# Differential attention with maxima of half rows, both maps combined on GpSimd, and V held stationary for two query tiles

## Chip, core, metric

The kernel runs on one core of one Trainium2 chip. The metric is the device time of one execution in microseconds, given as the median of several runs. In what follows TensorE is the matmul engine (PE, and PEld for its weight loads), VectorE is DVE, ScalarE is ACT, GpSimd is POOL, and SyncE (SP) issues the transfers. SBUF is the on-chip memory of 128 partitions, PSUM the smaller one that TensorE writes to; GpSimd doesn't work on PSUM.

## What is computed

One layer of an encoder over 2048 tokens of width 1024: a projection, differential attention with 4 heads, dilated attention with 8 heads, an output projection, an MLP and a gate. The change concerns the differential attention:

```python
def block(qblk):
    s = jnp.einsum('bhmqd,bhmkd->bhmqk', qblk.astype(jnp.float32) * scale, kf)
    pr = jax.nn.softmax(s, axis=-1)
    a = pr[:, :, 0] - lam * pr[:, :, 1]
    return jnp.einsum('bhqk,bhkd->bhqd', a, vf)
...
o = rms_norm(o, subln_g, SUBLN_EPS) * (1.0 - lam_init)
```

`m` counts the two maps of a head, `scale` is 64 ** -0.5, keys are 2048, and `vf` has 128 columns for a head.

## The kernel before

The kernel is a list of six phases, each with its own on-chip tiles and a barrier behind it. Every engine has its own program, written out by hand; the engines meet only at semaphores (`wait_ge`, `then_inc`), and each runs its program in order. Float32 products are made from halves: a value is split into `hi` (a rounded copy, on ScalarE) and `lo` (the rest, a subtraction on VectorE), and two or three products of halves are added (`matmul3`). Each product has its own load of the stationary operand.

`project_phase` ends with the query stage: it turns queries and keys (`products` on VectorE, `rope` on GpSimd, L368, two inputs in SBUF), splits them (`qk_hi` on ScalarE, L262; `qk_lo` on VectorE, L326, two inputs in SBUF) and stores both halves.

`differential_phase` has 64 steps (`STEPS`), one for each tile of 128 queries of each head; head by head, 16 tiles each. K and V of two heads are held, and queries for 8 tiles twice. Step `n` does this:

- TensorE: `score` makes the scores of a map, 128 queries by 2048 keys, into four PSUM banks of 512 (L753, L754), 8 products a map. The four banks are shared by all maps, so a map's banks are written again when ScalarE has read them.
- VectorE: `maximum` (L623) reduces 1024 columns of PSUM, twice a map; `negate` (L628) joins the two and multiplies by -scale.
- ScalarE: `exp` (L563) exponentiates 1024 columns, with the whole row's maximum as bias, into `e` in SBUF, and gives the sum of each half row.
- VectorE: `denominators` (L634), `reciprocals` (L640) and `coefficient` (L645, minus lambda times the ratio of the denominators); `combine` (L660) makes `a_row` = e of map 1 x coefficient + e of map 0 over 2048 columns, two inputs in SBUF.
- TensorE: `turn_a` (L763) transposes `a_row` in four groups of four blocks into two PSUM banks; `a_hi` on ScalarE (L570) and `a_lo` on VectorE (L666, one input in PSUM, one in SBUF) split each group and free its bank.
- TensorE: `values` (L775, L776) holds a block of the turned weights stationary and moves V's two halves side by side (256 columns) past it, 32 products a tile.
- ScalarE `part` (L577), VectorE `result` (L672), ScalarE `square` and `unit`, GpSimd `root` (L720 to L724, a power of one column) and `finish` (L730) scale and normalise the 128x128 result. SyncE stores it.

The stages overlap: scores of tile n+1 and n+2, the turning of tile n and the values of tiles n-1 and n-2 stand in one turn of TensorE's loop. The order of VectorE's loop is the one to follow: maximum of the next tile, denominators, `a_lo` of the tile before, reciprocals, maximum, coefficient, negate, `a_lo`, combine, maximum, maximum, negate, `a_lo`, `a_lo`, result, keep.

## Time and profile before

| | us |
|---|---|
| runs (3): median | 3828.11 |
| runs: lowest, highest | 3823.57, 3841.12 |
| profiled execution, its own time | 3841.16 |
| its span | 3839.0 |
| differential stage within the span, from its first transfer to the next stage's | 623.4 to 1421.6 |

| engine | busy us, whole span | share |
|---|---|---|
| TensorE | 3455.9 | 90% |
| VectorE | 1928.7 | 50% |
| ScalarE | 1337.9 | 35% |
| GpSimd | 663.8 | 17% |

A row of a timeline has the start, the length, the engine, the line, the operation and its tiles (out<-in, partitions x elements); behind it in brackets the idle time before it and what ended that. "x2" is two instructions in one row. An operation's start can lie a little before the end of its predecessor, because they are pipelined. Rows of groups have the count, the busy time, the mean length in ns, and the idle time before them. A "granted clock" of 1 is 2.4 GHz, 0.5 is 1.2 GHz.

### The profile page before, as it was taken

The numbers are of one execution on the slowest core, as the hardware profiler recorded it, in microseconds if no ns is written. First come the engines' busy times: TensorE is split into PE (matmuls) and PEld (weight loads), VectorE is DVE, ScalarE is ACT, GpSimd is POOL, SyncE is SP. The second block draws the span as 40 slices with busy tenths as digits, with TensorE's granted clock in tenths as the row PEclk, the third lists the DMA queues.
The fourth block names the chain that finished last, engine by engine and source line by source line (L and its number), as shares of the span: only waits on it lengthen the run. The fifth ranks groups of instructions, "written<-read, shape, count | busy, mean of one in ns | idle before, by whom it ended". The sixth has DMA issues, their size and how long they took to land. (4 is left out here: it accounts for less than half of the span.)

```text
span 3839.0 us, 51498 instructions
## 1 busy us (share of the span) xinstructions
PE 3455.9 (90%) x18272; PEld 2965.2 (77%) x18272; DVE 1928.7 (50%) x3626; ACT 1337.9 (35%) x2814; POOL 663.8 (17%) x760
## 2 busy tenths in 40 slices
PE   5999995888888869999489799999999999998698
PEld 5998884777777759999377688888888888887587
DVE  3214442889989958888344333333343333332333
ACT  3211111666666647776122221112221112111333
POOL 2013331011111110000121121122211222111122
PEclk8999997999999989999699899999999999999899
DMA  3333336212210026774454511111141111112332
GB/s 128 134 108 121 121 115 168 53 37 64 57 44 18 7 66 161 165 165 111 154 173 158 197 44 55 44 55 44 44 159 44 55 44 44 54 44 74 132 107 93
DMA packets 276374, 351.12 MB, mean 91 GB/s; under 512 B 74608, under 2 KB 204528, under 8 KB 270960
## 3 DMA queue, kind: packets, MB, share of 16 engines
q1 hardware_dynamic: 276208, 348.97, 30.5%
q8 instruction: 96, 1.57, 0.2%
q14 instruction: 70, 0.57, 0.1%
HBM read 247.86 MB, written 101.06 MB: 91 GB/s over the span
## 5 line engine op out<-in xcount | busy, mean ns | idle before, releaser
L1582 DVE TENSOR_TENSOR e_h<-e_down_acc,e_h 128x512 f32<-128x512 f32 x512 | 350.7, 691 | 850.1 <-PE e_down_acc L89 850.1
L87 PE MATMUL e_up_acc<-e_xt_hi,e_up_hi 128*128 128x512 f32 x1024 | 399.8, 390 | 20.7 <-DVE e_xt_lo L1559 20.7
L88 PE MATMUL e_up_acc<-e_xt_lo,e_up_hi 128*128 128x512 f32 x1024 | 399.5, 390 | 0.0
L89 PE MATMUL e_up_acc<-e_xt_hi,e_up_lo 128*128 128x512 f32 x1024 | 399.3, 390 | 0.0
L87 PE MATMUL e_down_acc<-e_down_hi,e_u_hi 128*128 128x512 f32 x1024 | 398.3, 389 | 0.0
L88 PE MATMUL e_down_acc<-e_down_lo,e_u_hi 128*128 128x512 f32 x1024 | 398.3, 389 | 0.0
L89 PE MATMUL e_down_acc<-e_down_hi,e_u_lo 128*128 128x512 f32 x1024 | 398.3, 389 | 0.0
L623 DVE TENSOR_REDUCE c_mx<-c_scores 128x1 f32<-128x1024 f32 x256 | 306.1, 1216 | 73.2 <-PE c_scores L754 73.2
L563 ACT ACTIVATE c_e<-c_scores,c_neg_max 128x1024 f32<-128x1024 f32 x256 | 283.4, 1113 | 87.9 <-DVE c_neg_max L628 87.9
L1602 POOL TENSOR_TENSOR e_sq<-e_r 128x512 f32<-128x512 f32 x128 | 133.7, 1045 | 1008.4 <-ACT e_r L1538 1008.4
L753 PE MATMUL c_scores<-c_kt_hi,c_qs 128*128 128x512 f32 x512 | 220.8, 431 | 51.1 <-DMA c_gain_in<-g_subln_dram 37.0
L775 PE MATMUL c_pv<-c_v_hl,c_at_hi 128*128 128x256 f32 x1024 | 249.3, 285 | 0.9 <-issue 0.9
L1532 ACT CAST e_down_hi<-e_down_raw 128x2048 fp32r<-128x2048 f32 x32 | 61.2, 1913 | 539.7 <-PE e_down_acc L89 538.1
L776 PE MATMUL c_pv<-c_v_hl,c_at_lo 128*128 128x256 f32 x1024 | 242.9, 280 | 0.0
L87 PEld LDWEIGHTS e_up_acc<-e_xt_hi,e_up_hi 128*128 128x128 f32 x1024 | 192.9, 188 | 61.6 <-issue 21.1
L763 PE MATMUL c_turned<-c_ident,c_a_row 128*128 128x128 f32 x1024 | 148.7, 279 | 101.2 <-DVE c_at_lo L666 100.1
L1047 PE MATMUL b_scores<-b_kt,b_qs 128*128 128x256 f32 x768 | 206.0, 400 | 25.6 <-DMA b_masks<-masks_dram 25.6
L763 PEld LDWEIGHTS c_turned<-c_ident,c_a_row 128*128 128x128 f32 x1024 | 121.6, 143 | 133.3 <-issue 115.5
L89 PEld LDWEIGHTS e_up_acc<-e_xt_hi,e_up_lo 128*128 128x128 f32 x1024 | 192.9, 188 | 40.2
L88 PEld LDWEIGHTS e_up_acc<-e_xt_lo,e_up_hi 128*128 128x128 f32 x1024 | 192.9, 188 | 40.1
L89 PEld LDWEIGHTS e_down_acc<-e_down_hi,e_u_lo 128*128 128x128 f32 x1024 | 192.2, 188 | 39.9
L88 PEld LDWEIGHTS e_down_acc<-e_down_lo,e_u_hi 128*128 128x128 f32 x1024 | 192.2, 188 | 39.9
(164 smaller groups left out, 7822.7 us busy)
## 6 DMA issues: line engine op xcount, KB each, us to landing
s_qkt<-a_hl SPq DMA_DIRECT2D x128, 256.0 KB, 2.8
e_up_raw<-w_up_dram SPq DMA_DIRECT2D x32, 1024.0 KB, 5.8
e_down_raw<-w_down_dram SPq DMA_DIRECT2D x32, 1024.0 KB, 4.9
s_v<-a_hl SPq DMA_DIRECT2D x64, 256.0 KB, 2.0
b_kt<-s_qkt SPq DMA_DIRECT2D x64, 256.0 KB, 10.9
a_w_raw<-w_in_dram SPq DMA_DIRECT2D x24, 512.0 KB, 5.6
d_nd<-s_nd SPq DMA_DIRECT2D x48, 256.0 KB, 4.2
a_rot<-x_dram SPq DMA_DIRECT2D x16, 512.0 KB, 3.8
```

What stands on the lines that cost most here:

```text
L87: nc.tensor.matmul(out, lhs_hi, rhs_hi, start=first, stop=False)
L88: nc.tensor.matmul(out, lhs_hi, rhs_lo, start=False, stop=False)
L89: return nc.tensor.matmul(out, lhs_lo, rhs_hi, start=False, stop=last)
L563: nc.scalar.activation(e[:, s, m, f * HALF:(f + 1) * HALF], scores[:, 2 * f:2 * f + 2].rearrange("p b k -> p (b k)"), ACT.Exp, bias=neg_ma ...
L623: nc.vector.tensor_reduce(mx[:, f:f + 1], scores[:, 2 * f:2 * f + 2].rearrange("p b k -> p (b k)"), AX.X, ALU.max).then_inc(S["mx"], 1)
L753: nc.tensor.matmul(scores[:, b], queries, kt_hi[:, h % 2, m, cols], start=True, stop=False)
L763: ins = nc.tensor.transpose(turned[:, g % 2, c * P:(c + 1) * P], a_row[:, n % 2, (4 * g + c) * P:(4 * g + c + 1) * P], ident[:])
L775: nc.tensor.matmul(pv[:, :2 * VD], at_hi[:, s, c], v, start=(c == 0), stop=False)
L776: ins = nc.tensor.matmul(pv[:, :2 * VD], at_lo[:, s, c], v, start=False, stop=(c == KT - 1))
L1047: ins = nc.tensor.matmul(dst, queries, keys, start=(u == 0), stop=(u == 1))
L1582: nc.vector.tensor_tensor(h[:, slot(z, t), cols], down_acc[:, k % 4], h[:, slot(z, t), cols], ALU.add).then_inc(S["h"], 1)
L1602: nc.gpsimd.tensor_tensor(sq[:, k % 2], r[:, k % 2], r[:, k % 2], ALU.mult).then_inc(S["sq"], 1)
```

## The change

- Each half row (1024 keys) of each map has its own maximum, negated by the reduction itself (`negate=True`), and is exponentiated with it at once. Afterwards the half rows are brought to the row's maximum by factors: `top_of` and `below_top` on VectorE, `correct` on ScalarE (an exponential of four columns), then `parts`, `denominators`, `reciprocals`, `shares`, `coefficients` on VectorE. The units are taken in the order map 0 and 1 of the first half, then of the second (`UNITS`).
- The factors (correction, one over the denominator, one or minus lambda) are multiplied in on GpSimd: `scale`, four times a tile over 128x1024 in place, and `combine`, twice a tile, e0 = e0 + e1 over 128x1024. For this there are three tiles of e for map 0 and two for map 1; `a_row` is gone.
- `values` handles two query tiles: V's halves are stationary and the weights of both tiles (256 columns) move, 48 products for two tiles. The result comes out turned; `o_out` on ScalarE copies it, `turn_back` on TensorE turns it, `square` and `root` (for both tiles at once) and `result` on VectorE normalise it, which also multiplies by the gain.
- V has one buffer, loaded by quarters; the queries are loaded for 4 tiles at a time; the first head's keys come in two halves.
- The factor 64 ** -0.5 is multiplied into the queries as they are split in `project_phase` and is left out of the exponentials, in the dilated phase and in the mixing too.
- TensorE's, ScalarE's and VectorE's loops are interleaved by quarters of a tile.

The core of the diff:

```diff
+            return (SCALE, 1.0)[QK_PAIRS[i // BLOCKS][2]]
...
+                        nc.scalar.activation(hl[:, 2 * ab], prod[:, 2 * ab], ACT.Copy, scale=factor(i)).then_inc(rope_hi, 1)
...
+                        nc.vector.scalar_tensor_tensor(out=hl[:, 2 * ab + 1], in0=prod[:, 2 * ab], scalar=factor(i),
+                                                       in1=hl[:, 2 * ab].bitcast(F32), op0=ALU.mult, op1=ALU.subtract
+                                                       ).then_inc(rope_lo, 1)
...
+    UNITS = tuple((m, f) for f in range(2) for m in range(2))
...
+                        sp.wait_ge(S["pv"], 8 * (h * PAIRS - 1) + 2 * g + 2)
...
+                    m, f = UNITS[u]
+                    act.wait_ge(S["negmax"], 4 * n + u + 1)
+                    if m == 0 and n >= 3:
+                        act.wait_ge(S["a_turned"], 4 * (n - 3) + 2 * f + 2)
+                    if m == 1 and n >= 2:
+                        act.wait_ge(S["a"], 2 * (n - 2) + f + 1)
+                    b = (4 * n + u) % 2
+                    nc.scalar.activation(e_of(n, m, f), scores[:, 2 * b:2 * b + 2].rearrange("p b k -> p (b k)"),
+                                         ACT.Exp, bias=neg_max[:, n % 2, m, f:f + 1],
+                                         accum_out=sums[:, n % 2, m, f:f + 1]).then_inc(S["exp"], 1)
...
+                    act.wait_ge(S["below"], n + 1)
...
+                                         below[:].rearrange("p m f -> p (m f)"), ACT.Exp).then_inc(S["corr"], 1)
...
+                for n in range(-2, STEPS + 4):
+                    j = n // 2 - 2
+                    closing = n % 2 == 0 and 0 <= j < STEPS // 2
+                    for q in range(4):
+                        if 0 <= n < STEPS:
+                            a_hi(n, q)
+                        if closing and q == 0:
+                            o_out(j)
+                        if n + 2 < STEPS:
+                            exp(n + 2, q)
+                        if closing and q >= 2:
+                            square(j, q - 2)
+                    if n + 2 < STEPS:
+                        correct(n + 2)
...
+                    nc.vector.tensor_reduce(neg_max[:, n % 2, m, f:f + 1],
+                                            scores[:, 2 * b:2 * b + 2].rearrange("p b k -> p (b k)"),
+                                            AX.X, ALU.max, negate=True).then_inc(S["negmax"], 1)
+                def top_of(n):
+                    dve.wait_ge(S["negmax"], 4 * n + 4)
+                    dve.wait_ge(S["below"], n)
+                    nc.vector.tensor_tensor(top[:], neg_max[:, n % 2, :, 0], neg_max[:, n % 2, :, 1],
+                                            ALU.min).then_inc(S["top"], 1)
+                def below_top(n):
+                    dve.wait_ge(S["top"], n + 1)
+                    dve.wait_ge(S["corr"], n)
+                    nc.vector.tensor_tensor(below[:], top[:].unsqueeze(2).to_broadcast([P, 2, 2]), neg_max[:, n % 2],
+                                            ALU.subtract).then_inc(S["below"], 1)
+                def parts(n):
+                    dve.wait_ge(S["corr"], n + 1)
+                    dve.wait_ge(S["den"], n)
+                    nc.vector.tensor_tensor(part[:], corr[:, n % 2], sums[:, n % 2], ALU.mult).then_inc(S["part"], 1)
...
+                    nc.vector.tensor_tensor(den[:], part[:, :, 0], part[:, :, 1], ALU.add).then_inc(S["den"], 1)
...
+                    nc.vector.tensor_tensor(share[:], rec[:], weights[:], ALU.mult).then_inc(S["share"], 1)
...
+                    nc.vector.tensor_tensor(coef[:, n % 2], corr[:, n % 2], share[:].unsqueeze(2).to_broadcast([P, 2, 2]),
...
+                    nc.vector.scalar_tensor_tensor(out=out[:, s], in0=o[:, s * P:(s + 1) * P], scalar=rstd[:, s:s + 1],
+                                                   in1=gain[:], op0=ALU.mult, op1=ALU.mult).then_inc(S["out"], 1)
...
+                    for q in range(4):
+                        if n + 2 < STEPS:
+                            maximum(n + 2, q)
+                        if chained:
+                            if q == 0:
+                                parts(n + 1)
+                            if q == 1:
+                                shares(n + 1)
+                        if 0 <= n < STEPS:
+                            a_lo(n, q)
+                        if chained:
+                            if q == 0:
+                                denominators(n + 1)
+                                reciprocals(n + 1)
+                            if q == 1:
+                                coefficients(n + 1)
+                        if closing and q < 2:
+                            result(j, q)
+                    if n + 2 < STEPS:
+                        top_of(n + 2)
+                        below_top(n + 2)
...
+                def scale(n, m, f):
+                    pool.wait_ge(S["coef"], n + 1)
+                    nc.gpsimd.tensor_scalar(e_of(n, m, f), e_of(n, m, f), coef[:, n % 2, m, f:f + 1], None,
+                                            ALU.mult).then_inc(S["scaled"], 1)
+                def combine(n, f):
+                    pool.wait_ge(S["scaled"], 4 * n + 3 + f)
+                    nc.gpsimd.tensor_tensor(e_of(n, 0, f), e_of(n, 0, f), e_of(n, 1, f), ALU.add).then_inc(S["a"], 1)
...
+                    nc.gpsimd.tensor_scalar(mean[:], ssq[:], 1.0 / VD, SUBLN_EPS, ALU.mult, ALU.add).then_inc(S["mean"], 1)
...
+                    nc.gpsimd.tensor_tensor(rstd[:], mean[:], half[:], ALU.pow).then_inc(S["rstd"], 1)
...
+                    if 0 <= n + 1 < STEPS:
+                        scale(n + 1, 0, 0)
+                        scale(n + 1, 1, 0)
+                        scale(n + 1, 0, 1)
+                        combine(n + 1, 0)
+                        scale(n + 1, 1, 1)
+                    if n % 2 == 0 and 0 <= j < STEPS // 2:
+                        root(j)
+                    if 0 <= n + 1 < STEPS:
+                        combine(n + 1, 1)
...
+                        pe.wait_ge(S["a_lo"], 4 * (2 * j + 1) + k // 2 + 1)
+                    for c in range(2 * k, 2 * k + 2):
+                        hi, lo = (t[:, s, c].rearrange("p s t -> p (s t)") for t in (at_hi, at_lo))
+                        ins = matmul3(nc, pv[:, :2 * P], v_hl[:, c, 0], v_hl[:, c, 1], hi, lo, c == 0, c == KT - 1)
...
+                    for q in range(4):
+                        if n + 2 < STEPS:
+                            score(n + 2, q)
+                        if 0 <= n < STEPS:
+                            turn(n, q)
+                        j = (n - 2) // 2
+                        if 0 <= j < STEPS // 2 and n >= 2:
+                            values(j, 4 * (n % 2) + q)
```

The functions that are replaced stand in the kernel printed above.

## Rows read from the trace of the kernel before

**Rows 1.** Busy time by engine, columns as headed, in the even middle of the stage.
```profile
core 0: us, PE busy (x) PEld busy (x) DVE busy (x) ACT busy (x) POOL busy (x), PEclk, DMA share, GB/s
700.00:1380.00 680.00, 583.03 (x3794) 497.54 (x3793) 613.64 (x952) 451.62 (x951) 90.80 (x236) 0.99 0.14 35
```

**Rows 2.** Timeline of VectorE over one step: start, length, line, operation, idle before.
```profile
1002.45 1.23 DVE L623 TENSOR_REDUCE c_mx<-c_scores 128x1 f32<-128x1024 f32 x1 [0.85 <-PE c_scores L754]
1003.59 0.15 DVE L634 TENSOR_TENSOR c_den<-c_sums 128x2 f32<-128x2 f32 x1
1003.65 0.68 DVE L666 TENSOR_TENSOR c_at_lo<-c_turned,c_at_hi 128x512 fp32r<-128x512 f32 x1
1004.25 0.15 DVE L640 RECIPROCAL c_rec<-c_den 128x2 f32<-128x2 f32 x1
1004.33 1.20 DVE L623 TENSOR_REDUCE c_mx<-c_scores 128x1 f32<-128x1024 f32 x1
1005.45 0.26 DVE L645 TENSOR_SCALAR c_coef<-c_den,c_neg_lam,c_rec 128x1 f32<-128x1 f32 x1
...
1012.32 0.34 DVE L672 SCALAR_TENSOR_TENSOR c_o<-c_pv,c_rec,c_o_part 128x128 f32<-128x128 f32 x1
...
1013.79 1.23 DVE L623 TENSOR_REDUCE c_mx<-c_scores 128x1 f32<-128x1024 f32 x1 [0.84 <-PE c_scores L754]
```

**Rows 3.** Waits of TensorE, 660 to 1400 us: total, times, longest.
```profile
PE c_turned L763 <- DVE c_at_lo L666: 100.1, 64, 1.6
```

**Rows 4.** Timeline of TensorE: scores, turns and values, to be read by starts.
```profile
703.75 0.40 PE L753 MATMUL c_scores<-c_kt_hi,c_qs 128*128 128x512 f32 x1
...
705.25 0.60 PE L763 MATMUL c_turned<-c_ident,c_a_row 128*128 128x128 f32 x4
705.60 0.37 PE L775 MATMUL c_pv<-c_v_hl,c_at_hi 128*128 128x256 f32 x1
...
705.92 0.28 PE L775 MATMUL c_pv<-c_v_hl,c_at_hi 128*128 128x256 f32 x1
706.04 0.28 PE L776 MATMUL c_pv<-c_v_hl,c_at_lo 128*128 128x256 f32 x1
```

**Rows 5.** Groups of ScalarE by shape, 620 to 1425 us: count, busy us, mean ns, idle.
```profile
L563 ACT ACTIVATE c_e<-c_scores,c_neg_max 128x1024 f32<-128x1024 f32 x256 | 283.4, 1113 | 87.9 <-DVE c_neg_max L628 87.9
```

**Rows 6.** Groups of GpSimd by shape, whole span: count, busy us, mean ns, idle.
```profile
L1602 POOL TENSOR_TENSOR e_sq<-e_r 128x512 f32<-128x512 f32 x128 | 133.7, 1045 | 1008.4 <-ACT e_r L1538 1008.4
...
L362 POOL TENSOR_TENSOR a_w_lo<-a_w_raw,a_w_hi 128x1024 fp32r<-128x1024 f32 x24 | 57.6, 2422 | 130.8 <-ACT a_w_hi L233 130.8
...
L356 POOL TENSOR_TENSOR a_rstd<-a_mean,a_half 128x1 f32<-128x1 f32 x16 | 8.8, 551 | 1.3
...
L351 POOL TENSOR_SCALAR a_mean<-a_ssq 128x1 f32<-128x1 f32 x16 | 3.1, 192 | 88.9 <-ACT a_junk L240 88.7
L1013 POOL MEMSET b_kt<- 128x1024 f32 x2 | 1.9, 952 | 3.1 <-POOLq L1948 3.0
```

**Rows 7.** Query stage: GpSimd's and VectorE's timelines, and L326's durations, min/median/max.
```profile
440.90 2.56 POOL L368 TENSOR_TENSOR a_prod<-a_prod 128x512 f32<-128x512 f32 x2 [8.32 <-DVE a_prod L319]
...
442.89 1.95 DVE L326 TENSOR_TENSOR a_hl<-a_prod,a_hl 128x512 fp32r<-128x512 f32 x2 [0.86 <-ACT a_hl L262]
...
L326 DVE TENSOR_TENSOR a_hl<-a_prod,a_hl x64: 692/889/1122, 279.7 to 618.2; 128x512 fp32r<-128x512 f32 x64
```

**Rows 8.** Timelines near the stage's end: VectorE's combining operation, GpSimd's power.
```profile
1383.86 2.34 DVE L660 SCALAR_TENSOR_TENSOR c_a_row<-c_e,c_coef 128x2048 f32<-128x2048 f32 x1
...
1384.13 2.48 POOL L724 TENSOR_TENSOR c_o_rstd<-c_o_mean,c_half 128x1 f32<-128x1 f32 x1
```

**Rows 9.** Timelines at the kernel's start: GpSimd's long pair, VectorE reading PSUM and SBUF.
```profile
11.39 5.28 POOL L362 TENSOR_TENSOR a_w_lo<-a_w_raw,a_w_hi 128x1024 fp32r<-128x1024 f32 x2 [0.56 <-ACT a_w_hi L233]
...
14.55 1.29 DVE L297 TENSOR_TENSOR a_xt_lo<-a_turned,a_xt_hi 128x512 fp32r<-128x512 f32 x2 [2.41 <-ACT a_xt_hi L246]
```

**Rows 10.** Busy times, granted clock, DMA at the stage's start (columns as rows 1).
```profile
623.00:651.00 28.00, 0.00 (x0) 0.00 (x0) 0.00 (x0) 0.00 (x0) 0.16 (x3) 0.50 0.98 210
```

## What the change should do to the time

> **What bounds the kernel now.** Only the differential stage (623 to 1421 us of the span of 3839.0) changes in its structure, so I read it alone: first busy time by engine, then one step of the bound engine, then who waits for it. In the even middle VectorE is busy 614 of 680 us, TensorE 583, ScalarE 452, GpSimd 91, at a granted clock of 0.99 [rows 1]. A step (one query tile of one head; there are 64) lasts 1013.79 - 1002.45 = 11.34 us by the start of its first maximum. In it VectorE idles once, 0.85 us, for scores [rows 2]; these come late because TensorE waits up to 1.6 us a step, 64 times, for the split of the turned weights on VectorE [rows 3]. So VectorE sets the step: 10.5 us of work and a loop through TensorE.
>
> I cost by starts, since neighbours overlap: a maximum 1005.45 - 1004.33 = 1.12 us, a split (c_at_lo) 1004.25 - 1003.65 = 0.60, a small independent operation 0.06 to 0.08, one that needs its predecessor's result its whole 0.15; a 128x128 scaling 0.34 long, some 0.26 [rows 2].
>
> **VectorE, its own work.** The combination over 2048 columns goes (2.34 us long [rows 8]), with the old coefficient, negations, copy and o. The four maxima and four splits stay: 4 x 1.12 + 4 x 0.60 = 6.9. Seven small operations come in their place (minimum of the half maxima, difference, parts, denominators, reciprocals, shares, coefficients): about 0.75. The final scaling is 0.26 for each tile. Sum 7.9 us, 2.6 below the 10.5 of now.
>
> **TensorE.** Scores are unchanged: six of them with a bank change took 705.25 - 703.75 = 1.50, so 16 take 4.0. Four turns take 0.35 (705.25 to 705.60), so 16 take 1.4. A 256-column product costs 706.04 - 705.92 = 0.12. Today 32 of them serve a tile; with V stationary 48 serve two tiles, so 24 a tile: 2.8 instead of 3.7 [rows 4]. With changes of kind in each quarter and the turns back, 9 us. Loads of V as stationary cost nothing more: there is one for each product now too. ScalarE loses two scalings of o, gains one copy per pair and an exponential of four columns; at 452 of 680 us, 7.5 a step, it has room [rows 1].
>
> **GpSimd.** This is what is new. It gets four scalings of 128x1024 in place by a per-partition number, and two additions of 128x1024. The addition has a row, the two-input subtraction of this size: 2.42 us on average, of which I use 2.40. A wide operation with one input has none. Lower end: the memset of this size, which only writes, 0.95. Upper end: 2.40 as for two inputs. Between them, squaring multiplies a tile with itself and reads it twice: (1.045 - 0.19) / 512 = 1.67 ns a column; read once, half of that, is 0.83, which is also the memset's rate. So I take 0.19 + 0.85 = 1.06, near the lower end [rows 6]. The sum is 4 x 1.06 + 2 x 2.40 = 9.0, with gaps 9.2, and every second step the root of the norm (0.19 + 0.55 and gaps, 0.9 with its wait) [rows 6]. 9.7 on average is more than TensorE's 9, and still below 11.34.
>
> **What GpSimd does to VectorE.** In the query stage GpSimd works from 440.90 to 443.46. VectorE's subtraction, both inputs in SBUF, starts at 442.89 and the pair ends at 444.84; of a pair one takes 0.69, the other 1.12 (the least and the most of that line). 442.89 + 1.12 = 444.01 = 443.46 + 0.55: it stood until GpSimd's instruction ended [rows 7]. The other way round, GpSimd's power of one column, begun at 1384.13 inside the combination that ran until 1386.20, lasted 2.48 [rows 8] instead of 0.55 [rows 6]. But two subtractions with one input in PSUM took an undisturbed 1.29 inside GpSimd's 11.39 to 16.67 [rows 9]. So an operation of VectorE that reads two SBUF tiles, and one of GpSimd that reads SBUF, exclude each other for whole instructions; maxima, splits and the final scaling (PSUM plus SBUF) don't. The Trainium skill (SBUF — State Buffer, Who interferes with whom) says so: an exclusive lock, held for a whole instruction, and only the shared ports contend; these rows agree. It makes no exception for small operations.
>
> The old stage had GpSimd almost empty. In the new one it works 9 us in a row, and six of VectorE's seven small operations read two SBUF tiles: all but the reciprocals. Behind each, in VectorE's order, stand the maxima, and behind these the exponentials, the next scores and everything else. One step, from the start of the coefficients at 0, which release GpSimd:
> - GpSimd: three scalings 0.26 to 3.44, addition from 3.52 to 5.92.
> - VectorE: maximum, split, maximum, split until 3.52; the minimum finds the addition and stands until 5.92, ends 6.07.
> - GpSimd's fourth scaling 6.07 to 7.13; the difference, which needs the minimum, stands until 7.13, ends 7.28. Maximum until 8.40.
> - GpSimd's second addition 7.28 to 9.68; parts stands until 9.68, ends 9.83. Split, denominators, reciprocals until 10.7; maximum 11.8, shares, split, and the next coefficients at 12.5.
>
> That is 7.9 of work (less the final scaling) and 4.8 of standing, partly in place of the idling of now. TensorE fits in: its four quarters of some 2.3 us need an exponential from two quarters before, 1.1 us long [rows 5]; the latest ends at 12.7, for scores (1.0) that are wanted at 14.2. The root adds 0.9 in every second step (it comes before the second addition), the final scaling 0.26 in the others: 13.1 on average. At 3.52 two requests fall together; if the minimum comes just ahead of the addition, the same layout gives 12.0, with the extras 12.6. I take the middle, 12.85.
>
> **The sum.** (12.85 - 11.34) x 64 = +97 us. The stage's start: for 28 us TensorE does nothing, since it waits for transfers of some 5 MB at 210 GB/s [rows 10]; half the first queries (0.5 MB) come later, -2 us. The 16 smaller key loads cost only issue time on SyncE's queue, which is ahead of the landings. V, now in one buffer, is reloaded by quarters of 0.5 MB at three changes of head, 2.4 us each at that rate, more than a step ahead of its use; uncovered, 3 x 10 us. In SyncE's queue these loads stand behind the stores of tiles that were done a step before, and the next keys behind them have 12 steps. The new waits of ScalarE for a free tile of weights concern tiles two and three steps old; its `correct` waits for the difference, so until 7.3 in the layout, and behind it the next turned group and exponential, which VectorE wants from 9.8 and allows from 8.4. The scale moved into the query stage rides on operations that are there anyway: the subtraction stays one pass, and VectorE idles there (0.86 ahead of it alone [rows 7]). Nothing for it, nor for the exponentials.
>
> The profiled execution took 3841.2 us, 13 above the median 3828.1. Its sum is 3841.2 + 95 = 3936, which is 3923 on the median.
>
> **Rivals.**
> - *Small operations aren't held* (the other side). If operations of two or four columns slip in, GpSimd's own 9.7 sets the step, with the loop through TensorE at most 10.3: 3828 - 64 x 1.35 = about 3740. For it: no row shows so small a two-input operation of VectorE beside a long one of GpSimd. Against it: the power of one column was held. It decides at 3.4 us of standing a step (11.34 - 7.9): below that the kernel is faster. 0.15.
> - *Held, but absorbed.* If TensorE paces VectorE anyway (9 against 7.9) and the small operations fall into GpSimd's gaps, two of three stands go and the step comes out where it is, 11.0 to 11.7: 3805 to 3850. 0.1.
> - *The wide scaling is slow.* At the rate of two reads, 0.19 + 1.70 = 1.89 us, GpSimd has 12.4 + 0.45 by itself and the layout, done again, gives 14.2, with the extras 14.7: +215, 4040. The Trainium skill (GPSIMD Engine Reference, 3.1 Elementwise) gives 1.03 cycles an element for short bodies, but 1.8 as the best of another loop, at 1.2 GHz: estimates of 0.9 and 1.5 us; by the latter the total would be near 4010. No row shows which. 0.15.
> - *The clock falls.* In the 28 us of waiting the granted clock was 0.50 [rows 10], which is 1.2 of 2.4 GHz. TensorE would be busy 9 of 12.85 against 583 of 680 now [rows 1]. Its idle pieces are below 3 us, so I give the long fall little: at half clock its 9 become 17, and 64 x 5.5 = +350. 0.03, within the tail.
>
> **How the numbers follow.** My forecast (held, narrow scaling, step 12.0 to 13.5, so 3868 to 3964) has 0.57: 3923. The range takes in the slow scaling above and most of the absorbed case below: 3815 to 4060. Half a per cent, 19 us, is about what can be told from no change. Faster: 0.15 and a third of the absorbed case, 0.18. Same: 0.05. Slower: 0.77.
>
> **What would show it.** VectorE's small two-input operations would show lengths of 1 to 2.5 us instead of 0.15, each ending just after an instruction of GpSimd; the reciprocals would stay at 0.15. GpSimd's scalings 1.06, additions 2.40. The products with V would number 1536 instead of 2048, and TensorE would wait for exponentials. Step near 12.85. I am wrong if these lengths are 0.15, or if GpSimd idles less than 2 us a step.

## The result and the profile after

The changed kernel took 4257.9 us (median of 4 runs, 4254.6 to 4261.0) against 3829.4 for the kernel before on the same chip: a ratio of 1.110, 95% interval 1.109 to 1.112. It is slower, as forecast, but by 428 us where I had said 95 (step 12.85 instead of 11.34), and outside the range. The profiled execution has a span of 4252.8 us. The difference lies in the differential stage: from 280 to 620 us, ahead of it, TensorE was busy 334.18 us before and 334.68 after, and the next stage issues its first transfer at 1415.4 us before and at 1840.6 after, 425 us later.

The stage's step went from 11.34 us to 11.34 + (4257.9 - 3829.4) / 64 = 18.0. All steps below are computed so: the difference to the kernel before on the same chip, divided by 64, plus 11.34. Counted in the traces by the maxima, steps come out up to 0.5 us longer (before 11.4, changed 18.2, the shortest one below 9.0 for 8.6), so these figures are good for differences, and not for what one step is to the tenth.

Busy time by engine in the even middle, the row that answers to [rows 1]:

```profile
core 0: us, PE busy (x) PEld busy (x) DVE busy (x) ACT busy (x) POOL busy (x), PEclk, DMA share, GB/s
700.00:1780.00 1080.00, 657.73 (x3366) 555.38 (x3366) 524.67 (x947) 438.71 (x916) 973.93 (x413) 0.78 0.09 24
```

GpSimd, busy 90.80 of 680 us before, is now busy 973.93 of 1080; TensorE and VectorE have fallen to 61% and 49%. The groups of GpSimd's and TensorE's operations on the page (count, busy us, mean ns, idle before) say which instruction it is; no row of before had the first:

```profile
L737 POOL TENSOR_SCALAR c_e<-c_e,c_coef 128x1024 f32<-128x1024 f32 x256 | 725.2, 2845 | 139.0 <-DVE c_coef L680 139.0
...
L795 PE MATMUL c_turned<-c_ident,c_e 128*128 128x128 f32 x1024 | 207.6, 339 | 430.6 <-POOL c_e L742 430.0
...
L742 POOL TENSOR_TENSOR c_e<-c_e 128x1024 f32<-128x1024 f32 x128 | 301.6, 2357 | 8.2
```

The addition costs 2.36, as its row of before said (2.42, [rows 6]). The scaling costs 2.84 us, not 1.06. The wait of TensorE's turns has changed its releaser: before, the split on VectorE, 100.1 us [rows 3]; now GpSimd's addition, 430.0.

GpSimd's timeline over one step (start, length, line, operation, idle before), to be read beside VectorE's, which answers to [rows 2]:

```profile
1097.33 8.49 POOL L737 TENSOR_SCALAR c_e<-c_e,c_coef 128x1024 f32<-128x1024 f32 x3 [0.79 <-DVE c_coef L680]
1105.90 2.34 POOL L742 TENSOR_TENSOR c_e<-c_e 128x1024 f32<-128x1024 f32 x1
1108.22 2.84 POOL L737 TENSOR_SCALAR c_e<-c_e,c_coef 128x1024 f32<-128x1024 f32 x1
1111.14 2.37 POOL L742 TENSOR_TENSOR c_e<-c_e 128x1024 f32<-128x1024 f32 x1
1116.08 8.49 POOL L737 TENSOR_SCALAR c_e<-c_e,c_coef 128x1024 f32<-128x1024 f32 x3 [2.57 <-DVE c_coef L680]
...
1130.74 2.39 POOL L742 TENSOR_TENSOR c_e<-c_e 128x1024 f32<-128x1024 f32 x1
```

VectorE's timeline in the same stretch, four of its small operations:

```profile
1101.08 0.20 DVE L647 TENSOR_TENSOR c_top<-c_neg_max 128x2 f32<-128x2 f32 x1
1101.31 0.16 DVE L653 TENSOR_TENSOR c_below<-c_top,c_neg_max 128x4 f32<-128x4 f32 x1
...
1122.51 0.34 DVE L659 TENSOR_TENSOR c_part<-c_corr,c_sums 128x4 f32<-128x4 f32 x1
...
1132.21 0.94 DVE L674 TENSOR_TENSOR c_share<-c_rec,c_weights 128x2 f32<-128x2 f32 x1
```

The reader is to see two things. GpSimd's own queue fills the step: from its first scaling to the end of its second addition 1113.51 - 1097.33 = 16.2 us without a root and 1133.13 - 1116.08 = 17.05 with one, 16.6 on average, and it idles only for coefficients (0.79 and 2.57). And VectorE's operations are held: the shares, begun inside an addition that ends at 1130.74 + 2.39 = 1133.13, end at 1133.15. But beside a scaling the hold is short. The parts begin at 1122.51, inside a scaling that began at 1116.08 + 2 x 2.83 = 1121.74, and end at 1122.85, which is 1.11 after its start. The difference at 1101.31 begins 1.15 after the start of a scaling (1097.33 + 2.83 = 1100.16) and isn't held at all. From 700 to 1350 us there are 23 small operations that a scaling lengthened, and all of them end 1.11 to 1.14 after its start. So after 1.1 of its 2.84 us the scaling no longer stands in VectorE's way.

### The profile page after: what moved, and what is told of

It is laid out like the page before. It is cut to its first block and busy times, and to the rows that moved or that the text cites. A ratio compares the mean times of both kernels' runs of the same rounds, so it can differ in the third digit from the quotient of the medians.

```text
span 4252.8 us, 51111 instructions
## 1 busy us (share of the span) xinstructions
PE 3522.2 (83%) x17824; PEld 3013.9 (71%) x17824; DVE 1832.8 (43%) x3626; ACT 1326.4 (31%) x2782; POOL 1614.7 (38%) x951
## 5 line engine op out<-in xcount | busy, mean ns | idle before, releaser
L737 POOL TENSOR_SCALAR c_e<-c_e,c_coef 128x1024 f32<-128x1024 f32 x256 | 725.2, 2845 | 139.0 <-DVE c_coef L680 139.0
L795 PE MATMUL c_turned<-c_ident,c_e 128*128 128x128 f32 x1024 | 207.6, 339 | 430.6 <-POOL c_e L742 430.0
L795 PEld LDWEIGHTS c_turned<-c_ident,c_e 128*128 128x128 f32 x1024 | 159.0, 176 | 496.2 <-POOL c_e L742 464.2
L686 DVE TENSOR_TENSOR c_at_lo<-c_turned,c_at_hi 128x512 fp32r<-128x512 f32 x256 | 175.5, 686 | 452.5 <-ACT c_at_hi L599 452.1
L640 DVE TENSOR_REDUCE c_neg_max<-c_scores 128x1 f32<-128x1024 f32 x256 | 312.5, 1221 | 120.9 <-PE c_scores L787 119.7
L599 ACT CAST c_at_hi<-c_turned 128x512 fp32r<-128x512 f32 x256 | 149.8, 585 | 656.8 <-PE c_turned L795 656.4
L742 POOL TENSOR_TENSOR c_e<-c_e 128x1024 f32<-128x1024 f32 x128 | 301.6, 2357 | 8.2
L786 PE MATMUL c_scores<-c_kt_hi,c_qs 128*128 128x512 f32 x512 | 238.7, 466 | 41.9 <-DMA c_gain_in<-g_subln_dram 34.5
L787 PE MATMUL c_scores<-c_kt_lo,c_qs 128*128 128x512 f32 x512 | 230.7, 451 | 0.0
```

Of the source, the lines that this page charges most:

```text
L640: nc.vector.tensor_reduce(neg_max[:, n % 2, m, f:f + 1], scores[:, 2 * b:2 * b + 2].rearrange("p b k -> p (b k)"), AX.X, ALU.max, negate=T ...
L737: nc.gpsimd.tensor_scalar(e_of(n, m, f), e_of(n, m, f), coef[:, n % 2, m, f:f + 1], None, ALU.mult).then_inc(S["scaled"], 1)
L742: nc.gpsimd.tensor_tensor(e_of(n, 0, f), e_of(n, 0, f), e_of(n, 1, f), ALU.add).then_inc(S["a"], 1)
L786: nc.tensor.matmul(bank, queries, kt_hi[:, h % 2, m, cols], start=True, stop=False)
L787: ins = nc.tensor.matmul(bank, queries, kt_lo[:, h % 2, m, cols], start=False, stop=True)
L795: ins = nc.tensor.transpose(turned[:, g % 2, c * P:(c + 1) * P], e0[:, n % 3, (4 * g + c) * P:(4 * g + c + 1) * P], ident[:])
```

## The experiments

Rows of kernels derived from the changed one bear its line numbers or nearly so. The edits are cut to their core: `e` stands for `e_of(n, m, f)`, and semaphores are left out.

### What the scaling costs, by its form

**scale8** scales 8 of the 1024 columns, **scale512** half of them; the rest stays unscaled.

```diff
-nc.gpsimd.tensor_scalar(e_of(n, m, f), e_of(n, m, f), coef[:, n % 2, m, f:f + 1], None, ALU.mult)
+nc.gpsimd.tensor_scalar(e_of(n, m, f)[:, :8], e_of(n, m, f)[:, :8], coef[:, n % 2, m, f:f + 1], None, ALU.mult)
```

> The changed kernel, but each of GpSimd's four scalings a tile covers 8 of 1024 columns, so most weights stay without their factor. The changed kernel has a step of 18.1 us, in which GpSimd works 4 x 2.84 + 2 x 2.36 us. Theory 1 (GpSimd's own queue sets the step): with 0.2 us a scaling GpSimd has 5.5 us and sets nothing; the step falls to what the other engines need, 9.1 to 10.5 us, time 3690 to 3775. Theory 2 (the standing of VectorE's small operations behind GpSimd is what costs): two additions a step still hold them, step 11 to 12.5, time 3810 to 3900. Theory 3 (the interleaving by quarters or V stationary cost time by themselves): the step stays above 12.5.

> The changed kernel with scalings over 512 of 1024 columns; the other half of the weights has no factor. A length linear in columns gives 0.19 + 1.33 = 1.52 us a scaling and GpSimd 11.2 us a step with its root; theory 1 with some 1.5 us of waiting for the coefficients gives a step of 12.7, 3915. Theory 2 gives the same GpSimd and up to 3 us of standing more, 4000 and above. The hold of a scaling on VectorE, 1.12 us in the changed kernel, should be some 0.65 if it is the reading of the columns, and stay 1.12 if it is a fixed cost.

Measured: scale8 3821.9 us, ratio 0.996 (0.995 to 0.998), step 11.1; scale512 3966.4 us, 1.034 (1.032 to 1.036), step 13.3. The first is where additions hold VectorE (theory 2), the second between the two theories. In scale512 three minima are lengthened beside a scaling, and all three end 0.68 to 0.69 after its start, so the hold isn't a fixed 1.12. **const_factor** puts the constant 0.5 in the place of the coefficient, **spread_factor** multiplies two tiles, the second being the coefficient spread with step 0:

```diff
-nc.gpsimd.tensor_scalar(e, e, coef[:, n % 2, m, f:f + 1], None, ALU.mult)
+nc.gpsimd.tensor_scalar(e, e, 0.5, None, ALU.mult)                                                 # const_factor
+nc.gpsimd.tensor_tensor(e, e, coef[:, n % 2, m, f:f + 1].to_broadcast([P, HALF]), ALU.mult)        # spread_factor
```

> The changed kernel with the constant 0.5 in place of the coefficient of each query, so the weights of the two maps are wrong, and the operation has the same form and size otherwise. If the factor's pointer is what makes a scaling 2.84 us instead of my 1.06, a scaling falls to about 1.1 us and the time towards 3925, my first layout. If the form of the operation costs that with any factor, 2.84 and 4258 stay.

> The changed kernel with each scaling as a product of two tiles, the second being the coefficient repeated over the columns with stride 0; the same result. Expected length that of the additions, 2.36 us. Theory 1: GpSimd has 6 x 2.36 = 14.2 us, 1.9 less, so the step 16.1 and 4135. Theory 2: each of the four now holds VectorE for its whole length instead of 1.12 us, the small operations stand longer, and most of the gain is lost: 4200 to 4300.

Measured: const_factor 4237.5 us, ratio 1.104; spread_factor 4037.8, 1.053 (1.051 to 1.054), step 14.5, less than either theory had, since a spread product takes 1.89 and not 2.36. **two_operations** gives the instruction a second operation that changes nothing, and **plain_copy** copies in place of scaling, so the factors are left out:

```diff
-nc.gpsimd.tensor_scalar(e, e, coef[:, n % 2, m, f:f + 1], None, ALU.mult)
+nc.gpsimd.tensor_scalar(e, e, coef[:, n % 2, m, f:f + 1], 0.0, ALU.mult, ALU.add)                  # two_operations
+nc.gpsimd.tensor_copy(e, e)                                                                        # plain_copy
```

> The changed kernel with a second arithmetic step, plus 0.0, in each of GpSimd's scalings; same result. A scaling took 2.84 us, of which VectorE was held for the first 1.12. If GpSimd works in passes over the tile, one for each arithmetic step or for reading and for the rest, the length grows by 0.9 or more, and the time by over 200. If the second step is free, 2.84 and 4258 stay.

> The changed kernel with a copy of each half row onto itself in place of the scaling; the weights lack their factors. One tile read, one written, no arithmetic. If one-input operations of GpSimd go at the rate that I had assumed, the copy takes 1.0 to 1.1 us and the time falls towards 3900. If it takes 2.5 or more, every one-input form is slower here than a product of two tiles.

Measured, one execution each, so without an interval: 3935.8 us (step 12.9) and 3894.8 (12.3). For two_operations I had expected the same length or a longer one; it became the shorter by 1.7 us. GpSimd's group of L737 between 700 and 1320 us, first in scale8:

```profile
L737 POOL TENSOR_SCALAR c_e<-c_e,c_coef 128x8 f32<-128x8 f32 x216 | 63.7, 307 | 221.9 <-DVE c_coef L680 221.9
```

The same group in scale512:

```profile
L737 POOL TENSOR_SCALAR c_e<-c_e,c_coef 128x512 f32<-128x512 f32 x181 | 281.3, 1566 | 99.1 <-DVE c_coef L680 99.1
```

The same group in const_factor:

```profile
L737 POOL TENSOR_SCALAR c_e<-c_e 128x1024 f32<-128x1024 f32 x139 | 382.7, 2770 | 56.0 <-DVE c_coef L680 56.0
```

The same group in spread_factor:

```profile
L737 POOL TENSOR_TENSOR c_e<-c_e,c_coef 128x1024 f32<-128x1024 f32 x168 | 314.5, 1893 | 85.4 <-DVE c_coef L680 85.4
```

The same group in two_operations:

```profile
L737 POOL TENSOR_SCALAR c_e<-c_e,c_coef 128x1024 f32<-128x1024 f32 x189 | 210.0, 1123 | 162.3 <-DVE c_coef L680 162.3
```

The same group in plain_copy:

```profile
L737 POOL COPY c_e<-c_e 128x1024 f32<-128x1024 f32 x198 | 200.3, 1041 | 161.8 <-DVE c_coef L680 161.8
```

The cost is one of columns: (2845 - 1566) / 512 = 2.50 ns each, (1566 - 307) / 504 = 2.50 as well. The number for each partition isn't the cause; a constant saves 0.07 us. Reading two tiles costs less (1.89) than reading one in this form. The same instruction with a second operation costs 1.12 us, with the same operands and the same result. So it is the form with one operation that is slow (tested with multiplication alone), and one added operation gives back 428 - 103 = 325 of the 428 us, by that one execution. What GpSimd does in that form the traces don't show; that stays open.

### Whether VectorE's small operations are held

**one_input_scale8** is scale8 with these operations rewritten so that each reads at most one tile in SBUF; **one_input** is the same rewriting with the scalings in full; **all8** is scale8 with additions over 8 columns too, so the stage does its work without most of the scaling and combining.

```diff
-nc.vector.tensor_tensor(top[:], neg_max[:, n % 2, :, 0], neg_max[:, n % 2, :, 1], ALU.min)
+nc.vector.tensor_reduce(top[:], neg_max[:, n % 2], AX.X, ALU.min)
-nc.vector.tensor_tensor(part[:], corr[:, n % 2], sums[:, n % 2], ALU.mult)
+nc.vector.tensor_scalar(part[:, m, f:f + 1], corr[:, n % 2, m, f:f + 1], sums[:, n % 2, m, f:f + 1], None, ALU.mult)   # 4 of them
+nc.vector.tensor_reduce(den[:], part[:], AX.X, ALU.add)
+nc.vector.tensor_scalar(coef[:, n % 2, m], corr[:, n % 2, m], rec[:, m:m + 1], weights[:, m:m + 1], ALU.mult, ALU.mult)  # 2
+nc.scalar.activation(corr[:, n % 2, m], neg_max[:, n % 2, m], ACT.Exp, bias=top[:, m:m + 1], scale=-1.0)   # difference in it
```

> The changed kernel with GpSimd's scalings and additions over 8 of 1024 columns; so most weights are those of map 0 alone, without factors. GpSimd has some 2 us a step and holds nothing longer than 0.3 us. With scalings of 8 columns alone the step was 11.1 us, where additions held VectorE's difference or denominators 2.2 us. If these holds are what keeps that kernel near 11 (theory H), the step now falls to TensorE's 9.1 to 9.8 us, time 3690 to 3740. If the interleaving or the turned result cost that time (theory I), it stays at 10.8 to 11.2, 3800 to 3820.

> Scalings of 8 columns as before (most weights without their factor), additions whole, and VectorE's six small operations rewritten so that none reads two SBUF tiles: the minimum and the denominators as reductions, the parts and the coefficients as products with a number per partition (nine small operations instead of seven), the difference taken inside ScalarE's exponential. Theory H: the small operations are never held, step 9.3 to 10.2, time 3705 to 3765. Theory I: no better than 3822. If products with a number per partition are held as well, they show 1 to 2 us beside an addition, and the time is as before or worse.

> The changed kernel with the same rewriting of VectorE's small operations and everything else as it is; the same result. Theory 1 (GpSimd's queue of 16.7 us sets the step, VectorE's standing lies beside it): no change, 4240 to 4270. Theory 2 (the standing is on the path): the step loses what the holds last, 0.3 to 2 us, 4130 to 4240.

Measured: all8 3666.9 us, ratio 0.956 (0.954 to 0.958), step 8.6; one_input_scale8 3693.1, 0.963 (0.961 to 0.965), step 9.0; one_input 4256.3, 1.109, step 17.8. The first two came out below the ranges of both their theories. In scale8, GpSimd's additions hold VectorE's difference and denominators (GpSimd's and VectorE's timelines, the second pair 15 us later):

```profile
1004.94 2.34 POOL L742 TENSOR_TENSOR c_e<-c_e 128x1024 f32<-128x1024 f32 x1
...
1005.03 2.26 DVE L653 TENSOR_TENSOR c_below<-c_top,c_neg_max 128x4 f32<-128x4 f32 x1
...
1019.99 2.39 POOL L742 TENSOR_TENSOR c_e<-c_e 128x1024 f32<-128x1024 f32 x1
...
1020.15 2.25 DVE L664 TENSOR_TENSOR c_den<-c_part 128x2 f32<-128x2 f32 x1
```

1005.03 + 2.26 = 1007.29 = 1004.94 + 2.34 + 0.01, and 1020.15 + 2.25 = 1022.40 = 1019.99 + 2.39 + 0.02. An operation of two columns stands for the whole addition. In one_input_scale8 the parts lie inside an addition and aren't held (the same two timelines):

```profile
1004.13 2.36 POOL L732 TENSOR_TENSOR c_e<-c_e 128x1024 f32<-128x1024 f32 x1
...
1005.43 0.57 DVE L655 TENSOR_SCALAR c_part<-c_corr,c_sums 128x1 f32<-128x1 f32 x4
```

That is worth 2.1 us a step (11.1 to 9.0), about 130 us in all. In scale8 the difference took 1.13 us on average and the denominators 1.20, where all8 has 0.16 and 0.15, together 2.0 us more, so the holds are as large as the gain. (The rewriting also takes the difference out of VectorE's order; all8, which keeps it, is no slower.) With the slow scalings it is worth nothing that the intervals tell apart (one_input 1.109, the changed kernel 1.110), because there the step is GpSimd's queue and its wait for coefficients. all8 gives the floor of the rest, with a step of 8.6 (busy time, columns as in [rows 1]):

```profile
700.00:1150.00 450.00, 426.24 (x2846) 375.81 (x2845) 403.89 (x799) 369.29 (x775) 99.53 (x347) 1.00 0.21 55
```

In these 450 us 50 tiles pass, 9.0 us each, in which TensorE is busy 8.5 and VectorE 8.1.

The holds of two_operations are the ones that I had laid out (timelines of GpSimd and VectorE):

```profile
1015.06 2.38 POOL L742 TENSOR_TENSOR c_e<-c_e 128x1024 f32<-128x1024 f32 x1
1017.43 1.11 POOL L737 TENSOR_SCALAR c_e<-c_e,c_coef 128x1024 f32<-128x1024 f32 x1
...
1019.45 2.38 POOL L742 TENSOR_TENSOR c_e<-c_e 128x1024 f32<-128x1024 f32 x1
...
1016.39 1.07 DVE L647 TENSOR_TENSOR c_top<-c_neg_max 128x2 f32<-128x2 f32 x1
1017.50 1.05 DVE L653 TENSOR_TENSOR c_below<-c_top,c_neg_max 128x4 f32<-128x4 f32 x1
...
1019.61 2.24 DVE L659 TENSOR_TENSOR c_part<-c_corr,c_sums 128x4 f32<-128x4 f32 x1
```

The minimum ends with the first addition (1017.44), the difference with the fourth scaling (1018.54), the parts with the second addition (1021.83). **two_operations_one_input** has both edits:

> The changed kernel with both edits at once: GpSimd's scalings carry a second operation (multiply by the coefficient, then add 0.0), and VectorE's small operations read at most one tile in SBUF (minimum and denominators as reductions, parts and coefficients as products with a number for each partition, the difference inside ScalarE's exponential). Theory (the one-operation form costs 2.84 us against 1.12, and what is left beyond GpSimd's own work is holding): nothing of VectorE is held, GpSimd has 4 x 1.12 + 2 x 2.37 + 0.5 and gaps = 9.9 a step, step 10.0 to 10.8, so 3740 to 3795 us; against two_operations alone (3936) at least 130 us less. Rival (the step of two_operations, 12.9 us, comes from the place of the coefficients in VectorE's order and not from holding): the reads don't matter, 3900 to 3940 us.

Measured: 3842.2 us, ratio 1.002 (1.001 to 1.003), step 11.5. Without the holds a step is 12.94 - 11.48 = 1.46 us shorter, 93 us in all. But the theory's 3740 to 3795 is missed: something else holds the step 1.6 us above GpSimd's 9.9.

### The loop through the coefficients

In two_operations_one_input GpSimd still waited for coefficients (waits, 700 to 1380 us: total, times, longest):

```profile
POOL c_e L727 <- DVE c_coef L673: 115.4, 58, 3.9
```

They stand in VectorE's order behind the second split of the tile before, which needs that tile's first addition, its turn and its high half. The loop is three scalings, addition, turn, high half, split, coefficients. The coefficients stand behind a maximum too, and in the changed kernel this one waits for scores that TensorE makes only after its long wait for the addition, at half clock (TensorE's timeline, a row of VectorE's, and busy time by engine with the granted clock third from the end):

```profile
1098.21 0.40 PE L786 MATMUL c_scores<-c_kt_hi,c_qs 128*128 128x512 f32 x1
1098.45 0.39 PE L787 MATMUL c_scores<-c_kt_lo,c_qs 128*128 128x512 f32 x1
...
1108.29 1.12 PE L795 MATMUL c_turned<-c_ident,c_e 128*128 128x128 f32 x4 [6.91 <-POOL c_e L742]
1111.81 0.63 PE L786 MATMUL c_scores<-c_kt_hi,c_qs 128*128 128x512 f32 x1
1112.23 0.63 PE L787 MATMUL c_scores<-c_kt_lo,c_qs 128*128 128x512 f32 x1
...
1113.75 1.23 DVE L640 TENSOR_REDUCE c_neg_max<-c_scores 128x1 f32<-128x1024 f32 x1 [2.73 <-PE c_scores L787]
...
1111.80:1113.50 1.70, 1.70 (x5) 1.22 (x5) 0.00 (x0) 0.00 (x0) 1.70 (x1) 0.50 0.00 0
```

After 6.91 us of idling a product starts 0.42 behind the one before it, where it was 0.24, and the granted clock is 0.50. So the four products of these scores take 1.70 us, and my estimate from the earlier starts is 4 x 0.24 = 1.0 at full clock.

The edit moves the coefficients, with all that they need, ahead of the first split and so ahead of that maximum; **early_coefficients** does that to the changed kernel, **two_operations_one_input_early** to the version above:

```diff
                         if chained and q == 0:
                             parts(n + 1)
+                            denominators(n + 1)
+                            reciprocals(n + 1)
+                            shares(n + 1)          # early_coefficients only
+                            coefficients(n + 1)
                         if 0 <= n < STEPS:
                             a_lo(n, q)
```

> The changed kernel with one move: parts, denominators, reciprocals, shares and coefficients of the next tile stand in VectorE's order ahead of the first split of the present tile (before: coefficients behind the second split, which needs the present tile's first addition, its turn and its high half). Theory (GpSimd's queue sets the step, and its wait for coefficients, 137 us in 62 steps of the middle, is on that path): the wait goes, the step falls from 18.1 to GpSimd's own 16.7, 64 x 1.4 = 90 us and at most 64 x 2.2 = 140 less than 4258: 4120 to 4170 us. Rival (the wait covers a stall that another loop would give anyway, through the exponentials and scores): 4240 to 4260.

> two_operations_one_input (3842 us, nothing held, GpSimd 9.6 of work a step, yet a step of 11.6) with the same move of the coefficients ahead of the splits. Theory (the loop coefficients, three scalings, first addition, turn, high half, splits, next coefficients sets the step: GpSimd waits 115.4 us in 58 steps of the middle for coefficients, 2.0 a step): the wait goes, the step falls to 9.9 to 10.6, 3735 to 3785 us. Rival (another loop, TensorE's turns waiting for additions, holds it): above 3820.

Measured: 4153.1 us, ratio 1.083 (1.082 to 1.085), step 16.3, GpSimd's own length; and 3760.6 us, 0.981 (0.979 to 0.983), step 10.2. Busy time in early_coefficients, columns as in [rows 1], shows GpSimd busy in 643 of 650 us:

```profile
700.00:1350.00 650.00, 418.45 (x2222) 351.35 (x2222) 402.23 (x623) 289.26 (x602) 643.34 (x273) 0.82 0.12 31
```

In it GpSimd's wait for coefficients is gone; in two_operations_one_input_early 24.5 us of it are left from 700 to 1350 us, 0.4 a step. Taken as differences to the kernel before, the loop was worth 428 - 318 = 110 us in the changed kernel and 9 + 74 = 83 us here. Of the three things that the move gets round (the split, the maximum, the slow scores) the runs don't say which was worth what.

In two_operations_one_input_early the coefficients, which read one tile in SBUF, are held after all (timelines of GpSimd and VectorE):

```profile
1013.04 2.40 POOL L729 TENSOR_TENSOR c_e<-c_e 128x1024 f32<-128x1024 f32 x1
...
1013.51 2.15 DVE L673 TENSOR_SCALAR c_coef<-c_corr,c_rec,c_weights 128x2 f32<-128x2 f32 x2
```

The pair takes 2.15 instead of 0.47 and ends 0.22 after the addition: the first of the two stands until its end. From 700 to 1300 us all of the 59 pairs but five begin inside an addition, and each of these ends 0.20 to 0.22 after it. In two_operations_one_input such an operation took 0.28 on average. **one_column_coefficients** writes the same numbers one column at a time:

```diff
-nc.vector.tensor_scalar(coef[:, n % 2, m], corr[:, n % 2, m], rec[:, m:m + 1], weights[:, m:m + 1], ALU.mult, ALU.mult)
+nc.vector.tensor_scalar(coef[:, n % 2, m, f:f + 1], corr[:, n % 2, m, f:f + 1], rec[:, m:m + 1], weights[:, m:m + 1], ALU.mult, ALU.mult)
```

> two_operations_one_input_early (3761 us) with the coefficients written by four operations of one column each instead of two of two columns; all the rest is the same. There the pair of two-column operations, which read one tile in SBUF, took 0.79 us on average instead of 0.28, because one that began beside an addition of GpSimd ended 0.2 us after it. Theory (a two-column tensor_scalar is held though it has one input in SBUF, a one-column one is not, as the parts, 0.20 us each in all runs): each takes 0.20 us, VectorE gains (87.8 - 59 x 4 x 0.2) / 59 = 0.7 us a step and GpSimd its coefficients that much earlier, so 15 to 50 us less: 3710 to 3745. Rival (what holds them is that the operation reads corr and two numbers for each partition, whatever its width): they are held too, 3760 or above.

Measured: 3728.1 us, ratio 0.972 (0.970 to 0.974), step 9.7: the fastest version that computes everything. The same place in its timelines:

```profile
718.44 2.40 POOL L731 TENSOR_TENSOR c_e<-c_e 128x1024 f32<-128x1024 f32 x1
...
718.89 0.82 DVE L674 TENSOR_SCALAR c_coef<-c_corr,c_rec,c_weights 128x1 f32<-128x1 f32 x4
```

Four operations of one column, begun inside an addition, take 0.82 together, as all 59 such groups do. So the width decides, not the operands. The Trainium skill (SBUF — State Buffer, Who interferes with whom) says that a tensor_scalar of VectorE can enter a mode that uses both port pairs and then contends with GpSimd; VectorE: DVE Perf Modes (Mode 2×_2P) has such a mode read the two halves of one tile at once. One column has no halves; that this is why it isn't held is my reading. The traces agree in what is held (two columns end 0.22 after the addition, one column takes 0.20); the ports they don't show.

### Work moved to ScalarE

**scalar_helps** lets ScalarE scale the first map, in the place of two of GpSimd's four scalings, with the spread product for the second; **scalar_helps_one_input** adds the one-input operations, **scalar_helps_both** the form with two operations (1.12) for the spread product (1.89).

```diff
+nc.scalar.activation(e_of(n, 0, f), e_of(n, 0, f), ACT.Copy, scale=coef[:, n % 2, 0, f:f + 1]).then_inc(S["scaled0"], 1)
```

> ScalarE multiplies map 0's two half rows by their factors in place, GpSimd only map 1's, as a product of two tiles with the factor repeated (1.89 us as measured), and adds; same result. GpSimd has 2 x 1.89 + 2 x 2.36 + 0.5 = 9.0 us, ScalarE some 7.2 + 2.1 = 9.3. Theory 1 with TensorE at 9.1: step 9.5 to 10.8, time 3715 to 3800. With the holds on the path (theory H), 1 to 2 us more: 3800 to 3900.

> ScalarE multiplies map 0's half rows by their factors, GpSimd map 1's with the factor repeated, and adds; VectorE's small operations read one SBUF tile each; same result as the changed kernel. Without the rewriting, ScalarE's help gave a step of 11.8 us and 3869, with VectorE's parts held up to 2.2 us. Theory H (the holds make the difference, as 129 us with scalings of 8 columns): nothing of VectorE is held, ScalarE's 9.4 and TensorE's 9.1 us set the step, 9.5 to 10.2, time 3720 to 3770, faster than the kernel before. If it stays above 3830, ScalarE's order is what holds it.

> scalar_helps_one_input (ScalarE scales the first map, VectorE's small operations read one tile in SBUF) with the second map's scalings on GpSimd in the form of two operations instead of the product with a broadcast factor: 1.12 us instead of 1.89. Theory A (GpSimd still sets the step there, 10.4 us): its work falls by 2 x 0.77 = 1.5 to 7.6 us a step, the step to 9.2 to 9.8, set by TensorE and ScalarE, so 3700 to 3740 us. Theory B (TensorE and ScalarE set it already): 3765 to 3780 us, as scalar_helps_one_input.

Measured: 3869.5 us, ratio 1.008 (1.006 to 1.011), step 11.8; 3775.2, 0.985 (0.983 to 0.987), step 10.4; 3772.1, 0.985 (0.982 to 0.987), step 10.4. The second is 5 us above its theory's range, the third as its theory B said. Holding costs 1.4 us a step here too. Once it is gone, 1.5 us less of GpSimd's work changes nothing. Then **scalar_helps_both_early** moves the coefficients ahead of the splits, and **scalar_helps_one_column** writes them by single columns and puts ScalarE's scalings one quarter earlier:

> scalar_helps_both (3772 us; GpSimd has 7.6 of work a step and waits 2.4 for coefficients) with the same move. Theory A (the same loop sets this step of 10.4 too): 3700 to 3740 us. Theory B (ScalarE, 9.4 of work with the scalings it took over, and TensorE set it): 3760 to 3780 us.

> scalar_helps_both_early (3845 us) with coefficients of one column each, and ScalarE's scalings of the first map one quarter earlier in its order (after the first and second exponential instead of the second and third). There GpSimd's second addition waited 3.3 us a step for ScalarE's scaling, which stands behind an exponential that waits for a maximum behind the held coefficients. Theory: both go, and TensorE and ScalarE (9.4 of work a step) set 9.6 to 10.4: 3715 to 3770 us. Rival (ScalarE's order of work is itself the bound, its scalings delay the exponentials wherever they stand): above 3800.

Measured: 3844.7 us, ratio 1.003 (1.002 to 1.004), a loss of 70 us that neither theory had; and 3748.5, 0.977 (0.975 to 0.980). In the first GpSimd waited for ScalarE (waits, 700 to 1350 us):

```profile
POOL c_e L739 <- ACT c_e L587: 182.8, 55, 4.2
ACT c_e L581 <- DVE c_neg_max L648: 94.8, 55, 3.2
```

ScalarE's second scaling stood behind an exponential that waited for a maximum, and that maximum behind coefficients held by an addition. Both were mended in one run, so how the 93 us that this gave back divide between them stays open.

## Where the prediction was right and wrong

**The step that failed** is the term "4 x 1.06" of GpSimd's sum. I had no row of a wide operation with one input on GpSimd and bounded it by the memset, 0.95, and by the two-input subtraction, 2.40. It was 2.84, above the upper bound; I had taken it for granted that reading one tile can't cost more than reading two. The one TENSOR_SCALAR row that I used, for the fixed 0.19 (L351 in [rows 6]), is of the fast form: in the kernel before it multiplies and adds. (My sum 0.19 + 0.85 is 1.04 and not 1.06, which changes nothing.) The value in between, worked out from the squaring, was right for two neighbours, 1.12 with two operations and 1.04 for a copy, but not for the form that the diff has. The term is 4 x 1.78 = 7.1 us a step too small. GpSimd's own length is then 16.6 instead of 9.7, past my layout's 12.85, so it sets the step. The rest is its wait for coefficients, 96.9 us in 60 waits between 700 and 1780 us, 1.6 a step, which early_coefficients took away (step 16.3). Of the 428 us lost, then, 110 are that loop; with the loop gone, 16.3 - 11.34 = 5.0 us a step, 318 us, are GpSimd's own queue.

**The rival "the wide scaling is slow"** had the mechanism, but with 1.89 us, which turned out to be the price of the spread product: spread_factor came to 4038, where I had said 4040 for that duration. In part that is luck: the kernel before took 3838 on that chip, so the loss was 200 us and not my 215. The Trainium skill (GPSIMD Engine Reference, 3.1 Elementwise) gave me estimates of 0.9 and 1.5 us; the first is near the copy's 1.04, and neither is near 2.84. (The total of 4010 that I gave for 1.5 doesn't follow from my layouts: between 3923 at 1.06 and 4040 at 1.89 it is about 3985.)

**Held small operations:** right, on a rule that I had from larger ones [rows 7, 8]. VectorE's operations of two and four columns stand for a whole addition (scale8), and the rival "not held" is dead. They cost 130 us in scale8 and 93 in two_operations, but nothing measurable in the kernel as changed.

**The layout of a step:** with the scaling that I assumed, two_operations gave 12.9 us and 3935.8 us of my 12.85 and 3923, and its timeline shows the three holds in the order of the layout. But the parts of it weigh otherwise than I thought. Without holds I put the step at 10.3 at most, and the kernel at 3740; two_operations_one_input took 11.5 and 3842. I had read the layout's last line, coefficients behind the second split, as a matter of holding. It is a loop of its own. So the agreement of the total, 12.9 with 12.85, is in part luck: holds that cost less than I had laid out, and a loop that I had left out.

**VectorE 7.9, TensorE 9:** about right. In all8 VectorE is busy 8.1 us a step and TensorE 8.5. The products with V were 3 x 512 = 1536, as said.

**The clock:** the granted clock fell from 0.99 [rows 1] to 0.78, a mean between its two levels, 1.2 and 2.4 GHz; TensorE idles up to 7.4 us at a time for additions, and behind an idle piece of 6.91 us it was at the lower one. I had named this with 3%, for the reason that idle pieces stay below 3 us, which no longer held. It has no part in the 318 us, since early_coefficients runs at GpSimd's own length with the clock at 0.82. It has one in the loop's 110 us, through the slow scores; how large wasn't measured.

**What the points of proof said:** "I am wrong if these lengths are 0.15" nearly misled. In the kernel as changed most are 0.15, and holding looks refuted; from 700 to 1350 us only 16 of 35 shares and 10 of 36 parts took over 0.4. Nearly all of the others met a scaling only after its first 1.1 us. The second sign, GpSimd idling less than 2 us a step, did come (106 of 1080 us, 1.8 a step), and it pointed at the term that failed.

## What to carry to other kernels

Price every wide instruction on GpSimd in the very form that it is issued in, or bound it openly from above: of five ways to copy or multiply 1024 columns the lengths were 1.04, 1.12, 1.89, 2.77 and 2.84 us. Wide work given to GpSimd can be paid for by VectorE's smallest operations, where they are on the path. In these runs reductions and one-column products with a number for each partition weren't held, operations with two inputs in SBUF and two-column products were. When a helper engine is started by coefficients, put what makes them ahead of everything that waits for that engine's last result.

## What was not expected of the hardware

- GpSimd's multiplication with one operation takes 2.50 ns a column and 0.3 us: 0.31 us at 8 columns, 1.57 at 512, 2.84 at 1024. With a second operation it takes 1.12 at 1024.
- VectorE is held by that slow form for 1.1 of its 2.84 us only, by an addition for all of its 2.36.
- A two-column tensor_scalar of VectorE with one tile in SBUF is held to the end of an addition of GpSimd (2.15 us for a pair instead of 0.47); four of one column in the same place take 0.82.
